# A two-block kernel on one core: ten of the twelve weight turns of the second attention taken from TensorE to VectorE and a pass through DRAM, and the level sums of the linear attention done earlier

## The chip, the cores and the metric

The kernel runs on one core of a Trainium2 chip. The metric is the time of one execution on the device, in microseconds; a lower time is better. All arithmetic is fp32; the large products are split into a high and a low part, so that each is three matmuls.

## What is computed

Two transformer blocks follow one another on 256 rows of 1024 columns. The first has a feed-forward part, a windowed attention with sinks beside a convolution, a second feed-forward part and a gated embedding. The second, cut to what matters here:

```python
h = rmsnorm(x) * (1 + sc2) + sh2
q_a, k_a, v_a, a_low, r_a, q_b, k_b, v_b, f_b, gate_a, gate_b = split(h @ w_in)
o_a = gla_chunked(q_a, k_a, v_a, log_a)          # linear attention, 4 heads of 128 x 256
o_b = fox_attention(q_b, k_b, v_b, logf)         # 16 heads of 64, causal:
#   s = q.k / 8 + F_t - F_s ; p = softmax(s) ; o = p @ v
merged = sigmoid(gate_a) * (o_a @ w_pa) + sigmoid(gate_b) * (o_b @ w_pb)
y = merged @ w_out
```

## The kernel before

**Stream of weight units.** All large products read weights as units of 128x1024 floats from DRAM. SyncE's queue loads them into a ring of eight buffers. ScalarE writes the high part `w_hi` (L676), VectorE the low part `w_lo` (L1194), TensorE multiplies (a unit of 512 columns is `col_unit`, L2029 to L2031, twelve matmuls) and frees the buffer. Each engine has one instruction list, written by hand, and steps through the units in the same order; `w.to(n)` in the lists of ScalarE and VectorE makes the parts of the units up to n + 1. Everything else is put between units.

**Second attention.** It runs in the sixteen steps of the last projection of the second mixer (the gate columns, a block of four units for each 512 columns; `for step in range(16)` at L1149, L1967, L2631). There are twelve groups of work, each with 128x512 scores in PSUM bank 4: groups 0 to 3 are four heads of the first 128 queries, groups 4 to 11 two heads of the second 128 queries with 256 keys. Group a has its scores at step a + 3:

- TensorE: `score_heads2` (L2285) adds q.k to the mask that ScalarE has copied into bank 4.
- VectorE: `heaviest2` takes the row maxima (L1533).
- ScalarE: `weigh2` takes the exponentials into `pr2` (L859) with their sums, then copies the next group's mask into bank 4 (L863).
- One step later TensorE turns the four 128x128 tiles of `pr2` into bank 5 (`turn_weights2`, L2295), ScalarE copies them to `pt2` (`take_turned2`, L870), and halfway through that step's unit TensorE multiplies them with the values, again into bank 5 (`weighted_values2`, L2306), as the stationary operand. VectorE scales and evicts the result (`take_values2`, L1545).

At steps 4 and 5 TensorE also turns the output of the linear attention.

**Linear attention.** Its scores are built up in nine steps, `gla_scores(i)` on TensorE and `masked(i)` on VectorE, one at the end and start of each block from 4 to 12 of the same projection. Steps 1 to 7 are levels of halving distance that are summed into `AT[:, 2]`; step 8 is the product between the two halves of the rows. When block 12 is over, TensorE turns the level sum (`turn_levels`, L2560) and issues step 8 (L2553). VectorE adds the sum to one diagonal tile, and the turned sum to the other (`add_levels`, two operations each, L1865 and L1866), and copies step 8 (L1846). `gla_values` (L2624), halfway through step 0 of the gate columns, needs all of that. Step 0 itself waits until ScalarE has evicted block 12 (L1127).

**GpSimd's queue** issues small loads, those of the modulation weights `ada` (L589), and in the second mixer the two rows of `Frow` (L665, L666). After these it has nothing until the last feed-forward part. The row-block layout that VectorE's transpose makes (32x32 blocks) is already used for the hidden units of the feed-forward parts (L1462), with DMAs on SyncE's queue that bring the blocks to their places.

## Time and profile before

| what | us |
|---|---|
| three runs | 1329.16, 1329.49, 1333.8 |
| median | 1329.49 |
| the profiled execution: its own time | 1329.29 |
| its span, from the first to the last instruction | 1327.5 |
| TensorE busy (share of the span) | 1311.3 (99%) |
| VectorE busy | 948.3 (71%) |
| ScalarE busy | 747.1 (56%) |
| GpSimd busy | 67.4 (5%) |

TensorE's clock was granted at 0.999 of full speed (2.4 GHz) over the span. The own time holds 1.8 us more than the span, which lies before the first and after the last instruction. In the rows, PE is TensorE's matmuls, PEld its weight loads (they overlap the matmuls), DVE is VectorE, ACT ScalarE, POOL GpSimd, SPq SyncE's queue of DMA issues; ps is PSUM. A matmul's duration in the rows includes its way through the pipeline, so that the spacing of the starts, not the duration, tells what it costs. The trace calls pr2, pt2 and gates2 by the names pr, pt and gates.

### The profile page before, as it was taken

What the parts mean: (1) busy time and instruction counts of PE and PEld (TensorE: products, weight loads), DVE (VectorE), ACT (ScalarE), POOL (GpSimd) and SP (SyncE); (2) the same over time, 40 slices, a digit from 0 to 9 for tenths busy, and PEclk for the clock granted to TensorE, in tenths of its full rate; (3) what the DMA queues carried; (4) which work ended last, traced back from release to release, by engine and by line L of the source; (5) the groups of instructions that cost most, each with busy time, mean ns of one, the idle gap of its engine ahead of it and who ended that gap; (6) DMA issues with size and microseconds to landing.
All of it is one profiled execution on the core that took longest, in us unless ns stands there. A gap on an engine that the chain in (4) does not pass through costs nothing.

```text
span 1327.5 us, 17135 instructions
## 1 busy us (share of the span) xinstructions
PE 1311.3 (99%) x6371; PEld 1094.0 (82%) x6371; DVE 948.3 (71%) x1352; ACT 747.1 (56%) x1149; POOL 67.4 (5%) x132
## 2 busy tenths in 40 slices
PE   9999999999999999999999999999999999999998
PEld 6888888888888888888788888889978888788886
DVE  6788877856656878887777888677866455766554
ACT  6454457567774544546744536766457663745452
POOL 3100100000000000110000010100000000000000
PEclk9999999999999999999999999999999999999999
DMA  9999966533375699895589996655644355567763
GB/s 288 317 297 310 319 215 191 174 114 109 96 254 184 212 277 311 306 338 160 173 252 298 294 309 183 204 175 173 172 133 119 104 175 173 159 207 217 219 197 105
DMA packets 185491, 282.45 MB, mean 213 GB/s; under 512 B 20386, under 2 KB 133258, under 8 KB 185408
## 3 DMA queue, kind: packets, MB, share of 16 engines
q1 hardware_dynamic: 172672, 238.22, 58.0%
q0 software_dynamic: 12576, 43.06, 9.8%
q8 instruction: 51, 0.84, 0.3%
q14 instruction: 32, 0.26, 0.1%
q10 hardware_dynamic: 160, 0.07, 0.1%
HBM read 268.66 MB, written 1.05 MB: 203 GB/s over the span
## 4 chain that ended last, share of the span: by engine, by line
PE 93%; DVE 3%; ACT 2%; DMA 1%; issue 0%; SPq 0%; DVEq 0%; POOL 0%; ACTq 0%
PE ps L2064 25%; PE ps L2029 16%; PE ps L2031 16%; PE ps L2030 16%; PE ps L2247 2%; PE ps L2043 1%; PE ps L2044 1%; PE ps L2045 1%; PE ps L2147 1%; PE ps L2149 1%; PE ps L2148 1%; PE ps L2079 1%; PE ps L2168 1%; PE ps L2322 1%; PE ps L2306 1%; PE ps L2285 1%
## 5 line engine op out<-in xcount | busy, mean ns | idle before, releaser
L1194 DVE TENSOR_TENSOR w_lo<-raw,w_hi 128x1024 fp32r<-128x1024 f32 (+2 forms) x431 | 514.2, 1213 | 218.1 <-ACT w_hi L676 216.8
L676 ACT ACTIVATE w_hi<-raw 128x1024 fp32r<-128x1024 f32 (+2 forms) x431 | 448.7, 1055 | 370.0 <-DMA raw<-in_w_gu_dram 100.0
L2029 PE MATMUL ps<-w_hi,a_hi 128*128 128x512 f32 (+1 forms) x976 | 386.4, 396 | 0.9 <-DVE w_lo L1194 0.9
L2031 PE MATMUL ps<-w_hi,a_lo 128*128 128x512 f32 (+1 forms) x976 | 378.7, 388 | 0.0
L2030 PE MATMUL ps<-w_lo,a_hi 128*128 128x512 f32 (+1 forms) x976 | 378.2, 387 | 0.0
L2031 PEld LDWEIGHTS ps<-w_hi,a_lo 128*128 128x128 f32 x976 | 183.3, 188 | 38.2
L2029 PEld LDWEIGHTS ps<-w_hi,a_hi 128*128 128x128 f32 x976 | 183.5, 188 | 36.8 <-DVE w_lo L1194 1.4
L2030 PEld LDWEIGHTS ps<-w_lo,a_hi 128*128 128x128 f32 x976 | 183.6, 188 | 35.7
L2064 PE MATMUL ps<-w_hi,hid_hi 128*128 128x512 f32 x300 | 93.1, 392 | 0.0
L2064 PE MATMUL ps<-w_hi,hid_lo 128*128 128x512 f32 x300 | 92.5, 389 | 0.0
L2064 PE MATMUL ps<-w_lo,hid_hi 128*128 128x512 f32 x300 | 92.4, 389 | 0.0
L1485 DVE SCALAR_TENSOR_TENSOR acc_m<-ada,csil,acc_m 128x1024 f32<-128x1024 f32 x63 | 80.7, 1281 | 4.7 <-DMA ada<-in_w_ada_dram 1.4
L2064 PEld LDWEIGHTS ps<-w_hi,hid_lo 128*128 128x128 f32 x300 | 56.3, 188 | 11.8
L2064 PEld LDWEIGHTS ps<-w_lo,hid_hi 128*128 128x128 f32 x300 | 56.3, 188 | 11.7
L2064 PEld LDWEIGHTS ps<-w_hi,hid_hi 128*128 128x128 f32 x300 | 55.7, 188 | 11.1
L589 POOL DMA_DIRECT2D ada<-in_w_ada_dram x72 | 38.3, 532 | 432.8 <-DVE acc_m L1485 269.3
L2064 PE MATMUL ps<-w_hi,a_hi 128*128 128x512 f32 x144 | 45.4, 396 | 0.6 <-DVE a_lo L1398 0.5
L2043 PE MATMUL ps<-a_hi,w_hi 128*128 128x256 f32 x160 | 45.9, 287 | 0.0
L2045 PE MATMUL ps<-a_lo,w_hi 128*128 128x256 f32 x160 | 45.3, 283 | 0.0
L2044 PE MATMUL ps<-a_hi,w_lo 128*128 128x256 f32 x160 | 45.3, 283 | 0.0
L2064 PE MATMUL ps<-w_lo,a_hi 128*128 128x512 f32 x144 | 44.4, 390 | 0.0
L2064 PE MATMUL ps<-w_hi,a_lo 128*128 128x512 f32 x144 | 44.4, 389 | 0.0
(438 smaller groups left out, 1597.0 us busy)
## 6 DMA issues: line engine op xcount, KB each, us to landing
raw<-in_ffn_wgu_dram SPq DMA_DIRECT2D x176, 256.0 KB, 4.7
raw<-in_w_in_dram SPq DMA_DIRECT2D x88, 512.0 KB, 3.7
raw<-in_w_gu_dram SPq DMA_DIRECT2D x176, 256.0 KB, 3.8
ada<-in_w_ada_dram POOLq DMA_DIRECT2D x72, 512.0 KB, 6.2
raw<-in_ffn_wdown_dram SPq DMA_DIRECT2D x44, 512.0 KB, 6.3
raw<-in_w_dn_dram SPq DMA_DIRECT2D x44, 512.0 KB, 4.6
raw<-in_w_in_dram SPq DMA_DIRECT2D x36, 256.0 KB, 3.1
raw<-in_w_out_dram SPq DMA_DIRECT2D x16, 512.0 KB, 3.7
```

What stands on the lines that cost most here:

```text
L589: pool.dma_start(ada[:, i % 3, :], w_ada[k, :, m * D:(m + 1) * D]).then_inc(sem(f"ada_landed{i % 3}"), 16)
L676: act.activation(w_hi[:, u % RING, 0:nk * n], raw[:, u % RING, 0:nk * n], ACT.Copy).then_inc(hi_ready, 1)
L1194: dve.tensor_tensor(w_lo[:, u % RING, 0:nk * n], raw[:, u % RING, 0:nk * n], w_hi[:, u % RING, 0:nk * n].bitcast(F32), ALU.subtract).then_ ...
L1485: ins = dve.scalar_tensor_tensor(acc_m[:, m % 2, :], ada[:, i % 3, :], csil[:, k:k + 1], acc_m[:, m % 2, :], ALU.mult, ALU.add)
L2029: pe.matmul(dst(t)[:, 0:n], a[0], slot(u, w_hi, kk, n), start=kc == 0, stop=False)
L2030: pe.matmul(dst(t)[:, 0:n], a[0], slot(u, w_lo, kk, n), start=False, stop=False)
L2031: i = pe.matmul(dst(t)[:, 0:n], a[1], slot(u, w_hi, kk, n), start=False, stop=kc == KC - 1)
L2043: pe.matmul(dst, hi, a_hi[:, kc, :], start=kc == 0 and q % 2 == 0, stop=False, skip_group_check=True)
L2044: pe.matmul(dst, lo, a_hi[:, kc, :], start=False, stop=False, skip_group_check=True)
L2045: i = pe.matmul(dst, hi, a_lo[:, kc, :], start=False, stop=kc == KC - 1, skip_group_check=True)
L2064: i = pe.matmul(ps[:, bank + 2 * t + n, :], a[x_], slot(u, w_, 0, D, 512 * n, 512 * (n + 1)), start=kc == 0 and x_ == 0 and w_ is w_hi, st ...
L2247: i = pe.matmul(ps[:, 2 * t + n, :], a[x_], slot(u + k, w_, 0, D, 512 * n, 512 * (n + 1)), start=k == 0 and x_ == 0 and w_ is w_hi, stop=F ...
```

## The change

Groups 0 to 9 of the second attention (`MOVED = 10`) are no longer turned on TensorE. In the step of their scores VectorE transposes `pr2` by 32x32 blocks into `blocks2`, written so that the four 128-column tiles lie interleaved. GpSimd's queue stores the 128x512 result in rows of the output tensor (which the kernel overwrites at its end), waits until the store has landed, and loads it back with four DMAs, one for each 32 partitions of `rows2`, where the blocks then stand as full transposes. TensorE reads them as the stationary operand, every fourth element, two steps after the scores and no longer one. Groups 10 and 11 keep the old way, with banks 6 and 7 for the turned tiles. ScalarE's evictions of turned tiles remain for those two. In the linear attention both `add_levels` move into block 12 on VectorE, and `turn_levels` between the second and the third unit of block 12 on TensorE. Semaphores of the two attentions are merged; this changes no order.

```diff
+        blocks2, _, _ = place("blocks2", [P, 2, 4, 32, 4], F32, KD0)
+        rows2, _, e = place("rows2", [P, 3, P, 4], F32, e)
+        def passed2(i):
+            return out[0, i % 2 * P:(i % 2 + 1) * P, 0:512]
+        MOVED = 10
...
+            for i in range(MOVED):
+                pool.wait_ge(sem("a2_blocks"), i + 1)
+                pool.dma_start(passed2(i), blocks2[:, i % 2].rearrange("p q v b -> p (q v b)")).then_inc(sem("a2_passed"), 16)
+                pool.wait_ge(sem("a2_passed"), 16 * (i + 1))
+                if i >= 1:
+                    pool.wait_ge(sem("a2_moved"), 64 * i)
+                if i >= 3:
+                    pool.wait_ge(sem("a2_values"), i - 2)
+                for q in range(4):
+                    dst = rows2[32 * q:32 * q + 32, i % 3].rearrange("p (i v) b -> p i (v b)", i=4)
+                    src = passed2(i).rearrange("(i u) (q n) -> q u i n", i=4, q=4)[q]
+                    pool.dma_start(dst, src).then_inc(sem("a2_moved"), 16)
...
-                if i >= 2:
-                    act.wait_ge(sem("a2_turned"), i - 1)
+                if 2 <= i < MOVED + 2:
+                    act.wait_ge(sem("a2_blocks"), i - 1)
...
-                if 1 <= a <= NG:
+                if MOVED < a <= NG:
                     take_turned2(a - 1)
...
+            def turn_blocks2(i):
+                dve.wait_ge(sem("a2_exp"), exps(i))
+                if i >= 2:
+                    dve.wait_ge(sem("a2_passed"), 16 * (i - 1))
+                dve.transpose(blocks2[:, i % 2].rearrange("p q v b -> p b q v"), pr2[:, i % 2, :].rearrange("p (b q u) -> p b q u", b=4, u=32))\
+                   .then_inc(sem("a2_blocks"), 1)
...
+                if b == 12:
+                    add_levels(0, AT[:, 2, :, :])
                 w.to(u1 + 2)
...
+                if b == 12:
+                    dve.wait_ge(sem("levels_turned"), 1)
+                    add_levels(1, by_head(ps[:, 5, :]))
                 w.to(u1 + 4)
...
                 w.to(G + step + 4)
-                if 1 <= a <= NG:
+                if 0 <= a < MOVED:
+                    turn_blocks2(a)
+                if 2 <= a < MOVED + 2:
+                    take_values2(a - 2)
+                if MOVED < a <= NG:
                     take_values2(a - 1)
...
             def weighted_values2(i):
                 n, h0, nh, nk = GROUPS[i]
+                if i < MOVED:
+                    pe.wait_ge(sem("a2_moved"), 64 * (i + 1))
+                    rows = [rows2[:, i % 3, :, c] for c in range(4)]
+                else:
+                    pe.wait_ge(sem("weights_taken"), NG + i - MOVED + 1)
+                    rows = [pt2[:, i % 2, c * P:(c + 1) * P] for c in range(4)]
                 if i >= 1:
                     pe.wait_ge(sem("a2_evict"), i)
...
+                    if b == 12 and i == 1:
+                        pe.wait_ge(sem("gla_masked"), NSTEP - 1)
+                        turn_levels()
...
-                if 1 <= a <= NG:
+                if MOVED < a <= NG:
                     turn_weights2(a - 1)
...
-                    if 1 <= a <= NG:
+                    if 2 <= a < MOVED + 2:
+                        weighted_values2(a - 2)
+                    if MOVED < a <= NG:
                         weighted_values2(a - 1)
```

## Rows read from the trace of the kernel before

**Rows 1.** The page: busy time of each engine and its share of the span.

```profile
PE 1311.3 (99%) x6371; PEld 1094.0 (82%) x6371; DVE 948.3 (71%) x1352; ACT 747.1 (56%) x1149; POOL 67.4 (5%) x132
```

**Rows 2.** Busy by stretch: us, engines, PEclk, DMA share, GB/s.

```profile
1000.00:1065.00 65.00, 64.69 (x383) 56.18 (x383) 35.91 (x74) 44.19 (x113) 0.00 (x0) 1.00 0.37 108
```

**Rows 3.** Groups by line: count | busy us, mean ns | idle before.

```profile
L2306 PEld LDWEIGHTS ps<-vb,pt 128*128 128x128 f32 x96 | 12.6, 191 | 1.0
...
L2295 PE MATMUL ps<-const,pr 128*128 128x128 f32 x48 | 7.3, 274 | 0.3 <-ACT pr L859 0.3
```

**Rows 4.** TensorE in time, steps 13, 14: start us, us, engine, line.

```profile
1051.41 1.03 PE L2285 MATMUL ps<-kb,qb 66*128 66x256 f32 x4
1052.09 0.58 PE L2029 MATMUL ps<-w_hi,a_hi 128*128 128x512 f32 x1
...
1053.65 1.00 PE L2306 MATMUL ps<-vb,pt 128*128 128x64 f32 x8
1054.45 0.48 PE L2029 MATMUL ps<-w_hi,a_hi 128*128 128x512 f32 x1
...
1055.92 0.60 PE L2295 MATMUL ps<-const,pr 128*128 128x128 f32 x4
...
1060.87 0.60 PE L2295 MATMUL ps<-const,pr 128*128 128x128 f32 x4
```

**Rows 5.** VectorE and ScalarE in order of time, steps 13 and 14.

```profile
1054.75 0.29 DVE L1545 TENSOR_TENSOR oat<-ps,st 128x128 f32<-128x128 f32 x1 [0.18 <-PE ps L2306]
1057.43 0.69 DVE L1533 TENSOR_REDUCE st<-ps 128x2 f32<-128x512 f32 x1 [2.38 <-PE ps L2285]
...
1058.82 0.47 ACT L859 ACTIVATE pr<-ps,st 128x256 f32<-128x256 f32 x1
```

**Rows 6.** Steps 3 and 4 in order of time, three engines.

```profile
1003.77 1.22 DVE L1194 TENSOR_TENSOR w_lo<-raw,w_hi 128x1024 fp32r<-128x1024 f32 x1
...
1004.24 0.60 ACT L863 ACTIVATE ps<-const 128x512 f32<-128x512 f32 x1
...
1004.89 1.16 PE L2285 MATMUL ps<-kb,qb 66*128 66x128 f32 x8
```

**Rows 7.** End of linear attention, in time; brackets: idle, its releaser.

```profile
983.25 0.60 PE L2560 MATMUL ps<-const,AT 128*128 128x128 f32 x4
983.45 1.09 ACT L1127 ACTIVATE vb<-ps 128x512 f32<-128x512 f32 x2 [0.47 <-PE ps L2031]
...
983.69 1.06 PE L2553 MATMUL ps<-qk 128*128 128x128 f32 x8
...
984.59 0.50 PE L2029 MATMUL ps<-w_hi,a_hi 128*128 128x512 f32 x1
...
987.05 0.69 DVE L1846 COPY AT<-ps 128x512 f32<-128x512 f32 x1
...
987.80 1.99 PE L2624 MATMUL ps<-va,AT 128*128 128x256 f32 x8 [1.56 <-DVE AT L1846]
```

**Rows 8.** VectorE's block transposes, one of two tiles: ns min/median/max.

```profile
L1462 DVE STREAM_TRANSPOSE turned_even<-hid x24: 711/712/715, 29.8 to 1252.9; 128x512 f32<-128x512 f32 x24
```

**Rows 9.** VectorE and GpSimd in order of time, from 869 us.

```profile
869.18 0.74 DVE L1923 TENSOR_SCALAR Frow<-ps 16x256 f32<-16x256 f32 x2
...
870.22 0.50 POOL L665 DMA_DIRECT2D qb<-Frow  x1 [32.95 <-DVE Frow L1923]
```

**Rows 10.** GpSimd's DMA issues, one line: ns min/median/max.

```profile
L589 POOL DMA_DIRECT2D ada<-in_w_ada_dram x72: 530/530/554, 33.1 to 793.1; - x72
```

**Rows 11.** DMA issues: count, KB each, median us issue to landing.

```profile
out_dram<-x SPq DMA_DIRECT2D x4, 256.0 KB, 2.0
...
glam<-shape_constants_dram POOLq DMA_DIRECT2D x1, 512.0 KB, 3.9
...
pin<-in_p_dram POOLq DMA_DIRECT2D x1, 256.0 KB, 4.6
...
qb<-Frow POOLq DMA_DIRECT2D x1, 16.0 KB, 2.1
```

More of the change, by code:

```diff
@@ L865, in take_turned2 @@
             def take_turned2(i):
-                act.wait_ge(sem("a2_turned"), i + 1)
-                if i >= 2:
-                    act.wait_ge(sem("a2_values"), i - 1)
-                act.activation(pt2[:, i % 2, :], ps[:, 5, :], ACT.Copy).then_inc(sem("a2_pt"), 1)
+                act.wait_ge(sem("weights_turned"), NG + i - MOVED + 1)
+                act.activation(pt2[:, i % 2, :], ps[:, 6 + i % 2, :], ACT.Copy).then_inc(sem("weights_taken"), 1)
             def split_hi(k):
@@ L930, in weigh @@
                     act.wait_ge(sem("qs_ready"), 2)
-                act.wait_ge(sem("a1_bias"), i + 1)
+                act.wait_ge(sem("bias_ready"), i + 1)
                 if i >= 2:
-                    act.wait_ge(sem("a1_turned"), i - 1)
+                    act.wait_ge(sem("weights_turned"), i - 1)
                 if i >= 4:
@@ L1553, in heaviest @@
                     dve.wait_ge(sem("qs_ready"), 2)
-                dve.wait_ge(sem("a1_scores"), i + 1)
+                dve.wait_ge(sem("scores_ready"), i + 1)
                 src = ps[:, 4, 0:nh * L].rearrange("p (h k) -> p h k", k=L)
@@ L2286, in score_heads2, with weighted_values2 @@
                                    skip_group_check=True)
-                i_.then_inc(sem("a2_scores"), 1)
+                i_.then_inc(sem("scores_ready"), 1)
             def turn_weights2(i):
                 pe.wait_ge(sem("a2_exp"), exps(i))
+                pe.wait_ge(sem("act_lo"), 8 * TURN["oa"] + 8)
+                for q in range(4):
+                    i_ = pe.transpose(ps[:, 6 + i % 2, q * P:(q + 1) * P], pr2[:, i % 2, q * P:(q + 1) * P], ident)
+                i_.then_inc(sem("weights_turned"), 1)
+            def weighted_values2(i):
+                n, h0, nh, nk = GROUPS[i]
+                if i < MOVED:
[4 more added lines that the diff above has]
+                    rows = [pt2[:, i % 2, c * P:(c + 1) * P] for c in range(4)]
                 if i >= 1:
                     pe.wait_ge(sem("a2_evict"), i)
-                for q in range(4):
-                    i_ = pe.transpose(ps[:, 5, q * P:(q + 1) * P], pr2[:, i % 2, q * P:(q + 1) * P], ident)
-                i_.then_inc(sem("a2_turned"), 1)
-            def weighted_values2(i):
-                n, h0, nh, nk = GROUPS[i]
-                pe.wait_ge(sem("a2_pt"), i + 1)
                 for q in range(nh):
@@ L2304, in weighted_values2 @@
                     for k in range(nk):
-                        c = (q * nk + k) * P
-                        i_ = pe.matmul(ps[:, 5, q * HD:(q + 1) * HD], pt2[:, i % 2, c:c + P], vb[:, k, hh * HD:(hh + 1) * HD],
+                        i_ = pe.matmul(ps[:, 5, q * HD:(q + 1) * HD], rows[q * nk + k], vb[:, k, hh * HD:(hh + 1) * HD],
                                        start=k == 0, stop=k == nk - 1)
@@ L2323, in score_heads @@
                                    start=False, stop=True, skip_group_check=True)
-                i_.then_inc(sem("a1_scores"), 1)
+                i_.then_inc(sem("scores_ready"), 1)
             def turn_weights(i):
@@ L2332, in turn_weights @@
                     i_ = pe.transpose(ps[:, 5, q * P:(q + 1) * P], pr[:, i % 2, q * P:(q + 1) * P], ident)
-                i_.then_inc(sem("a1_turned"), 1)
+                i_.then_inc(sem("weights_turned"), 1)
             def weighted_values(i):
                 n, h0, nh, nk = GROUPS[i]
-                pe.wait_ge(sem("a1_pt"), i + 1)
+                pe.wait_ge(sem("weights_taken"), i + 1)
                 for q in range(nh):
```

19 lines of the change are left out of this document (7 added, 12 removed).

## The prediction

> **What bounds the kernel.** I began with the page: TensorE is busy 99% of the span [rows 1]. A change can then win only by giving TensorE less to do or by closing one of its few gaps, and it loses wherever TensorE has to wait for something new. Next I took the busy times by stretch for the sixteen steps of the second block's gate columns, where the second attention runs: TensorE 64.69 of 65 us, VectorE 35.91, ScalarE 44.19, GpSimd nothing, DMA engines 0.37 [rows 2]. TensorE is the bound, and GpSimd and the DMA engines look free. The groups by line give the price of what is removed [rows 3], the order in time gives one steady step [rows 4] with the other engines beside it [rows 5], the first step [rows 6] and the end of the linear attention [rows 7]. For the new path there is nothing in this stretch, so I read, from the whole run, VectorE's block transposes, GpSimd's DMA issues and the list of landings [rows 8 to 11].
>
> One steady step [rows 4]: scores from 1051.41 to 1052.09 (0.68 us), half a weight unit to 1053.65 (1.56), weighted values to 1054.45 (0.81), the other half to 1055.92 (1.46), transposes to the next scores. The step before ends where the next begins, 1055.92 to 1060.87: 4.95 us.
>
> **Removed from TensorE.** Four transposes for each of ten groups. In the steady step they fill 1055.92 to 1056.36, as the rest of the step adds up to 4.51 of 4.95: 0.44 us a group (the group's 274 ns a transpose is pipelined duration, not spacing [rows 3]). Ten would be 4.4. The first gives nothing: at 1004.89 the scores of group 1 start right after ScalarE's mask copy ends (1004.24 + 0.60 = 1004.84) [rows 6], so without the transposes TensorE waits for that copy instead. Nine groups give 9 x 0.44 = 3.9 us. ScalarE's ten evictions go too, but ScalarE is not the bound: nothing.
>
> **Moved on TensorE.** The weighted values of groups 0 to 9 come one step later. The same matmuls, so no cost, but step 14 now holds those of group 9 and of group 10, and both write bank 5: the second waits until VectorE has evicted the first. In step 13 VectorE's eviction ends at 1054.75 + 0.29 = 1055.04, 0.6 after the values end at 1054.45 [rows 4, 5]; behind a whole weight subtraction (1.22 us [rows 6]) it would be about 1.2. I take **0.9 us lost**, between the two.
>
> **Added to VectorE.** Ten 128x512 block transposes. The nearest row is 712 ns for the same shape [rows 8]; this one writes each element 16 bytes from the last, which no row shows, so 0.71 to 1.42 (double). It waits for the group's last exponential, and behind it stand the eviction and the next group's maximum. Scores at 1056.36 give the maximum at 1057.43 (+1.07) and the last exponential until 1059.29 (+2.93) [rows 5]; transposed by +3.75, evicted by +4.4. The next maximum starts at 4.51 + 1.07 = +5.58, so 1.1 us is spare and the transposes are hidden; at 1.42 still just.
>
> **Added on GpSimd: the part that decides.** A group is one 256 KB store to DRAM, a wait until it has landed, and four 64 KB loads, all issued by one queue in order. The loads of a group also wait for those of the group before (landed by then, while a load takes under 3 us) and for a buffer. So GpSimd cannot take groups faster than
>
> period P = store landing (Lw) + wake (0.30) + 4 issues.
>
> Wake: VectorE finished Frow at 869.92 and GpSimd issued at 870.22 [rows 9]. An issue: 0.53 us, 72 of them between 530 and 554 ns [rows 10]. Lw is not shown. From below, 2.0 us: the 256 KB output stores on SyncE's queue when nothing else moves. On GpSimd's queue 16 KB landed in 2.1 us and 512 KB in 3.9; a straight line gives 3.0 at 256 KB. From above, 4.6 us: the 256 KB load of pin on that queue beside other traffic [rows 11]. Here the DMA engines are about a third busy [rows 2], so I take **2.7**, nearer the quiet rows. P = 2.7 + 0.3 + 2.12 = 5.12 us. TensorE's step without the transposes is 4.51. GpSimd is slower and sets the pace, and the pace is even slower than the 4.95 of before.
>
> The end of that chain: group 0's exponentials are done while VectorE is in the subtraction that ends at 1003.77 + 1.22 = 1004.99 [rows 6]; transposed 1005.7; first store issued 1006.0. Ten periods later the queue is at 1057.2, the last load was issued 0.53 before that and lands Lr later. Lr for 64 KB: the same line gives 2.3, from 2.1 (16 KB) to 3.9; I take 2.4 since four overlap. Landed 1059.07, TensorE starts group 9's values at 1059.2, then 0.81 + 0.9 + 0.81 + 1.46 brings step 14 to its end at 1063.2. Before it ended at 1060.87 [rows 4]. **Attention: +2.3 us.** While GpSimd paces, 0.1 us on Lw is worth 1.0 us on the end.
>
> The loads of weights share the DMA engines with this. Each is asked for several steps ahead and the engines are far from full, so nothing; uncovered, a late unit would stop TensorE directly. The DMAs pass nothing: GpSimd's next work lies after the attention, and the output rows used as scratch are written by SyncE at the very end.
>
> **Linear attention.** Before: the four level transposes at 983.25, scores of the last level to 984.59, step 0 begins, then gla_values waits 1.56 us until VectorE has done four level operations and the copy of 987.05 to 987.74 [rows 7]. After: the transposes sit inside block 12 (0.44 moved, not saved), the four operations of 0.69 run under its matmuls, where VectorE has pauses, and only the copy follows. It takes 0.69 and is done before the first half of step 0 is. So the 1.56 goes, but something else is late: step 0 also needs ScalarE's evictions of block 12, which start when its matmuls end, 983.45 to 984.54. Now they end 0.44 later, at 985.0, against 984.59 where step 0 began. 1.56 - 0.4 = **1.2 us gained**. Bounds: 0 (VectorE late with its subtractions) and 1.6.
>
> **Sum.** +2.3 - 1.2 = +1.1 on the profiled execution's own 1329.29 us (span 1327.5): 1330.4. The median of the runs is 0.2 above it, so **1330.6 us**. By 0.5% (6.65 us, about what a measurement of this kernel tells from no change) that is no change.
>
> **Rivals.**
>
> *The round trip keeps up.* With Lw at or under 2.3, as the output stores suggest, TensorE waits only for group 0 (0.2 us at Lw 2.1): -3.9 + 0.9 + 0.2 - 1.2 = -4.0, 1325.5 us. For it: stores may be quicker than loads. Against it: both GpSimd rows beyond 16 KB.
>
> *The store lands late: slower.* The same chain, but Lw 3.5 with the weight loads' bursts in the way, as pin's 4.6 hints [rows 11]: +1.1 + 8 = +9.1, 1338.6 us. It decides from Lw = 3.25 on (1.1 + 5.5 = 6.6). Against it: pin met other traffic that is mostly absent here.
>
> *The stationary operand is slow to load.* Group rows now lie interleaved, so each stationary column is 16 bytes after the last. In this stretch the value matmuls are spaced 0.1 us apart and their weight loads take about 0.19 each [rows 3, 4], so little hides a longer load. If the load takes twice as long, values cost 1.62 a group, a step 5.32: above GpSimd's 5.12, so the two do not add, TensorE is simply the slower one. 8.1 more on the -4.0 of the keeping-up case, with part of group 0's wait on top: about +5, 1334.6. At three times, +13. No row here has such a stride. The Trainium skill ("SBUF — State Buffer", Specifications) says SBUF has 16-byte lines and wants at least two hits on a line for full bandwidth; by it this stride of one hit a line is the bad case, on the stationary operand and on VectorE's write both. No trace here shows it.
>
> *GpSimd is held up while it issues.* If two of a group's five issues each waited 0.6 us for a VectorE operation, +12 on the chain, 1342.6. Against it: 72 issues at 530 to 554 ns beside a busy VectorE [rows 10]. The Trainium skill ("SBUF — State Buffer", SBUF: two separate sides) describes VectorE's two-port modes locking GpSimd out of writing descriptors; by that rule it is possible, and the trace shows no sign of it.
>
> **Chances.** The forecast (GpSimd paces, Lw 2.4 to 3.2, own range 1327.6 to 1335.6) 0.42; keeps up 0.20; late store 0.16; slow stationary load 0.17, a third of it at the triple price; held up 0.05. Faster by over 0.5% would need 6.65 us, and all gains together (4.4 + 1.6) do not reach it: 0.03 for what I overlook. Slower by over 0.5%: 0.16 + 0.06 + 0.05 and the edge of the forecast, 0.30. Same: 0.67. The range for 8 in 10 goes from 1325.0, just under the keeping-up case, to 1341.0, which takes in Lw up to 3.7 and leaves out the triple load and most of the held-up case.
>
> **What would show it.** On GpSimd, 50 issues, the stores 5.1 us apart with no pause but the wait for landing; store landing 2.7, load landing 2.4. On TensorE, no idle before the scores, a wait of about 1.5 before group 0's values and about 0.6 before each later group's, by DMA; in step 14 a wait by VectorE near 0.9; gla_values without its 1.56, and about 0.4 before step 0. Values at 0.1 us apart and weight loads at 0.19 refute the slow load. VectorE's block transpose at 0.71 or above tells the stride's price there. I am wrong if Lw is off by more than a few tenths, which weighs ten times over, or if the interleaved rows cost TensorE time of their own.

## The result and the profile after

The changed kernel takes 1348.01 us (median of 6 runs, 1346.66 to 1354.3) against 1329.59 for the kernel before on the same chip: ratio 1.014, 95% interval [1.0124, 1.0155], 18.4 us slower. The forecast was 1330.6 with a range of 1325.0 to 1341.0. It was wrong: the time lies 7 us above the range. The profiled execution took 1351.19 us (span 1349.4). Line numbers below are those of each kernel's own program, so the values of a group are L2306 before and L2341 after, the scores L2285 and L2315, a weight unit's matmuls L2029 to L2031 and L2059 to L2061.

As before, the busy times by stretch come first; the stretch of the sixteen gate steps now ends near 1087. The columns are us, busy time of PE, PEld, DVE, ACT, POOL, granted clock as a share of 2.4 GHz, share of the DMA engines and GB/s.

```profile
1010.00:1020.00 10.00, 7.93 (x37) 6.66 (x35) 4.57 (x10) 3.99 (x15) 4.97 (x10) 0.83 0.54 162
...
1030.00:1040.00 10.00, 6.84 (x25) 5.61 (x24) 3.53 (x6) 4.51 (x9) 5.46 (x10) 0.79 0.51 150
...
1070.00:1080.00 10.00, 6.39 (x25) 5.49 (x24) 2.62 (x7) 1.60 (x5) 0.61 (x2) 0.67 0.24 70
1080.00:1090.00 10.00, 9.70 (x45) 7.89 (x45) 3.01 (x7) 3.73 (x8) 0.00 (x0) 0.82 0.37 107
```

Before, TensorE was busy 64.69 of 65 us at full clock here [rows 2]. Now these three windows from 1010 to 1080 have 2 to 3.6 us without TensorE, and in the same windows the clock is down to 0.67 to 0.83: for a part of them TensorE ran at the lower of its two levels, 1.2 GHz. Next, who waited for whom on TensorE, 984 to 1090 us: us in total, times, longest.

```profile
PE ps L2341 <- DMA rows<-out_dram: 8.3, 3, 3.2
PE ps L2315 <- ACT ps L881: 1.0, 1, 1.0
PE ps L2341 <- DVE oat L1569: 0.5, 1, 0.5
```

The groups of the new path in 984 to 1088 us (count | busy, mean ns of one | idle before):

```profile
L684 POOL DMA_DIRECT2D rows<-out_dram x40 | 21.8, 551 | 30.4 <-DMA out_dram<-blocks 29.7 <-issue 0.6
L2341 PEld LDWEIGHTS ps<-vb,rows 128*128 128x128 f32 x80 | 19.4, 325 | 10.1 <-DMA rows<-out_dram 9.8
L1557 DVE STREAM_TRANSPOSE blocks<-pr 128x512 f32<-128x512 f32 x10 | 11.1, 1115 | 1.3 <-ACT pr L877 1.3
```

A stationary load of landed rows takes 325 ns where it took 191 [rows 3]; a block transpose that writes every 16 bytes takes 1115 ns where 712 is the kernel's other price [rows 8]. GpSimd's issue is 0.55 us as expected [rows 10]. And TensorE in order of time, around the first long wait:

```profile
1010.82 0.40 PE L2061 MATMUL ps<-w_hi,a_lo 128*128 128x512 f32 x1
1013.29 2.08 PE L2341 MATMUL ps<-vb,rows 128*128 128x64 f32 x8 [2.07 <-DMA rows<-out_dram]
1015.18 0.60 PE L2059 MATMUL ps<-w_hi,a_hi 128*128 128x512 f32 x1
1015.58 0.63 PE L2060 MATMUL ps<-w_lo,a_hi 128*128 128x512 f32 x1
1016.00 0.63 PE L2061 MATMUL ps<-w_hi,a_lo 128*128 128x512 f32 x1
...
1019.93 0.48 PE L2059 MATMUL ps<-w_hi,a_hi 128*128 128x512 f32 x1
1020.25 0.40 PE L2060 MATMUL ps<-w_lo,a_hi 128*128 128x512 f32 x1
1020.48 0.39 PE L2061 MATMUL ps<-w_hi,a_lo 128*128 128x512 f32 x1
```

Behind a wait of 2.07 us the matmuls start 0.42 us apart (1015.58 to 1016.00) instead of 0.23 (1020.25 to 1020.48), until 1019. The other two waits, 3.16 and 3.06 us, are followed by the same picture; the lower clock is granted for 3.4, 6.8 and 10.2 us. Last, GpSimd in order of time, and one weight load of SyncE:

```profile
1016.13 0.56 POOL L675 DMA_DIRECT2D out_dram<-blocks  x1
1018.75 2.17 POOL L684 DMA_DIRECT2D rows<-out_dram  x4 [2.06 <-DMA out_dram<-blocks]
1025.02 0.58 POOL L675 DMA_DIRECT2D out_dram<-blocks  x1 [4.10 <-DVE blocks L1557]
1031.31 2.31 POOL L684 DMA_DIRECT2D rows<-out_dram  x4 [5.71 <-DMA out_dram<-blocks]
```

```profile
1024.71 0.37 SPq L541 DMA_DIRECT2D raw<-in_w_in_dram  x1
```

The store of 1016.13 lets GpSimd go on 2.6 us later, that of 1025.02 6.3 us later. The second one was issued 0.31 us behind a 512 KB weight load. That store is what TensorE's 3.16 us at 1035.46 come from. Over the ten stores the landing has this spread:

```profile
DMA to landing us min/median/max: 2.3/2.4/6.0
```

The three waits do not have one origin. Group 0's store (1005.62) landed in the quick 2.34 us. Its last row load was issued at 1009.9, so even a landing of 2.3 us would have come 1 us after TensorE was ready at 1011.2; it took 3.4 us, which makes the 2.07. The wait before group 9's values closes a chain of two late stores and a late row load, here in the order of the chain that ends there (start, us):

```profile
1056.53 4.15 DMA out_dram<-blocks
...
1063.13 5.03 DMA out_dram<-blocks
...
1070.06 4.20 DMA rows<-out_dram
...
1074.31 1.90 PE ps L2341 x7
```

The linear attention did what the prediction said:

```profile
984.34 1.05 PE L2588 MATMUL ps<-qk 128*128 128x128 f32 x8
985.67 0.50 PE L2059 MATMUL ps<-w_hi,a_hi 128*128 128x512 f32 x1 [0.28 <-ACT vb L1143]
...
987.17 1.02 PE L2660 MATMUL ps<-va,AT 128*128 128x256 f32 x4
```

The 1.56 us ahead of the values [rows 7] are gone and 0.28 stand before step 0.

### The profile page after: what moved, and what is told of

It is laid out like the page before. It is cut to its first block, busy times and chain, and to the rows that moved or that the text cites. A ratio compares the mean times of both kernels' runs of the same rounds, so it can differ in the third digit from the quotient of the medians.

```text
span 1349.4 us, 17117 instructions
## 1 busy us (share of the span) xinstructions
PE 1324.3 (98%) x6331; PEld 1104.8 (82%) x6331; DVE 957.5 (71%) x1362; ACT 741.1 (55%) x1139; POOL 94.5 (7%) x182
## 4 chain that ended last, share of the span: by engine, by line
PE 89%; DMA 4%; DVE 3%; POOL 1%; ACT 1%; issue 1%; SPq 0%; DVEq 0%; ACTq 0%; POOLq 0%
PE ps L2094 25%; PE ps L2059 15%; PE ps L2061 15%; PE ps L2060 15%; DMA out_dram<-blocks 2%; PE ps L2277 2%; PE ps L2073 1%; PE ps L2074 1%; PE ps L2075 1%; POOL rows L684 1%; PE ps L2177 1%; PE ps L2179 1%; PE ps L2178 1%; PE ps L2109 1%; PE ps L2198 1%
## 5 line engine op out<-in xcount | busy, mean ns | idle before, releaser
L2059 PE MATMUL ps<-w_hi,a_hi 128*128 128x512 f32 (+1 forms) x976 | 388.5, 398 | 1.3 <-DVE w_lo L1210 1.0
L2061 PE MATMUL ps<-w_hi,a_lo 128*128 128x512 f32 (+1 forms) x976 | 380.4, 390 | 0.0
L2059 PEld LDWEIGHTS ps<-w_hi,a_hi 128*128 128x128 f32 x976 | 184.8, 189 | 38.1 <-DVE w_lo L1210 1.5
L2061 PEld LDWEIGHTS ps<-w_hi,a_lo 128*128 128x128 f32 x976 | 184.4, 189 | 38.4
```

The source lines that it names most:

```text
L2059: pe.matmul(dst(t)[:, 0:n], a[0], slot(u, w_hi, kk, n), start=kc == 0, stop=False)
L2061: i = pe.matmul(dst(t)[:, 0:n], a[1], slot(u, w_hi, kk, n), start=False, stop=kc == KC - 1)
```

## The experiments

For every kernel I read the same distance in TensorE's order of time, from the scores of group 0 to the transposes of the second attention's output ("attention" in the table): 64.8 us before, 87.2 after. The profiled executions differ by 21.9 us (the changed kernel's is 3 us above its median), so all of the loss lies there. "Waits" are TensorE's for landed rows (us, times), "low" is the time at the lower clock inside the stretch, "store" the landing of the ten stores (min/median/max).

| kernel | median us | ratio [95%] | attention | waits | low | store |
|---|---|---|---|---|---|---|
| before | 1329.6 | | 64.8 | | 0 | |
| after | 1348.0 | 1.0140 [1.0124, 1.0155] | 87.2 | 8.3, 3 | 20.5 | 2.3/2.4/6.0 |
| levels | 1328.95 | 0.9993 [0.9984, 1.0002] | 64.8 | | 0 | |
| attn | 1349.5 | 1.0149 [1.0131, 1.0167] | 82.7 | 7.5, 3 | 10.2 | 2.3/3.0/4.7 |
| strided | 1340.0 | 1.0075 [1.0059, 1.0090] | 75.3 | | 0 | |
| contig | 1350.0 | 1.0142 [1.0123, 1.0160] | 86.4 | 12.5, 4 | 27.3 | 2.3/3.5/4.7 |
| fill | 1343.8 | 1.0110 [1.0082, 1.0138] | 82.5 | 5.7, 3 | 10.2 | 2.3/2.9/4.5 |
| traffic | 1328.6 | 0.9993 [0.9984, 1.0003] | 64.9 | | 0 | 2.3/2.9/4.8 |
| gated | 1342.3 | 1.0097 [1.0082, 1.0112] | 78.7 | 3.6, 3 | 6.8 | 2.3/3.1/4.1 |
| gated_contig | 1340.7 | 1.0085 [1.0069, 1.0102] | 76.0 | 10.1, 9 | 3.4 | 2.3/3.1/4.2 |
| sp_loads | 1341.8 | 1.0089 [1.0074, 1.0104] | 78.1 | 3.6, 3 | 6.8 | 2.3/2.8/5.9 |
| late | 1335.3 | 1.0046 [1.0032, 1.0061] | 70.0 | 0 | 0 | 2.3/2.9/4.5 |
| late_contig | 1331.9 | 1.0011 [1.0000, 1.0022] | 65.1 | 2.2, 3 | 0 | 2.3/2.9/4.6 |
| late_scalar | 1339.7 | 1.0079 [1.0062, 1.0096] | 76.7 | 9.8, 9 | 6.8 | 2.3/2.9/5.1 |
| lead3 | 1336.6 | 1.0050 [1.0034, 1.0065] | 72.3 | 0 | 3.4 | 2.3/2.5/4.6 |
| lead3_scalar | 1335.6 | 1.0044 [1.0032, 1.0057] | 70.5 | 0 | 6.8 | 2.3/2.8/4.6 |

Each ratio is against runs of the kernel before on the same chip (medians 1329.35 to 1329.75 us). The attention, waits, low and store columns are of one profiled execution each, the median of 4 to 11 runs, and the two can differ by some us (attn: profiled 1347.66, median 1349.5), so a single trace places the loss only to about that. In late_scalar the waits are those for ScalarE's copy of the rows.

**The two halves of the change (levels, attn).** levels is the kernel before with only this:

```diff
+                if b == 12:
+                    add_levels(0, AT[:, 2, :, :])
...
+                    if b == 12 and i == 1:
+                        pe.wait_ge(sem("gla_masked"), NSTEP - 1)
+                        turn_levels()
...
-                    if b - 4 == NSTEP - 1:
-                        turn_levels()
```

> The kernel before with the level sums of the linear attention inside the last block and nothing else changed. Theory: the level sums are worth what the trace after shows, gla_values 1.3 us earlier after the last unit of block 12, at the price of nothing: about 1328.4 us, 0.999 of before. TensorE idle before gla_values gone, about 0.3 us before step 0. Rival: the gain is given back later (the first scores wait for the same chain on VectorE), 1329.6 us.

1328.95, and 1328.89 with 0.9991 [0.9982, 1.0000] in a second trial (levels2, below): 0.8 us under the kernel before on the same chip both times, while both intervals reach up to no change. A small gain is likely and not shown. attn is the changed kernel with the level sums put back after block 12 (the same lines the other way round).

> The changed kernel with the level sums put back behind the last block, so the attention part alone. Theory: this part carries the whole loss, about 1.3 us above the changed kernel: 1349 us (+19.7). Rival: part of the loss comes from the level sums, which delay VectorE: then this is at or under 1347 us.

1349.5: the whole loss is the attention's, whatever the linear attention does.

**The stride alone (strided).** The kernel before, but ScalarE writes its copy of the turned weights interleaved and TensorE reads them with 16 bytes from column to column. No store, no load, no wait.

```diff
-                act.activation(pt2[:, i % 2, :], ps[:, 5, :], ACT.Copy)
+                act.activation(pt2[:, i % 2, :].rearrange("p (v b) -> p b v", b=4), ps[:, 5, :].rearrange("p (b v) -> p b v", b=4), ACT.Copy)
...
-                        c = (q * nk + k) * P
+                        c = q * nk + k
```

> The kernel before with one edit: ScalarE writes the turned tiles into pt2 interleaved by four, and TensorE reads them as stationary operand with that stride of 16 bytes; no DMA, no block transposes. Theory: the stride alone costs 0.85 us for each of twelve groups, 10.2 us: 1339.8 us, weight loads at about 325 ns, clock as before. Rival: the slow weight loads of the changed kernel come from rows that a DMA has written or from traffic at the same time: then 1330 us and loads at 191 ns. ScalarE's strided write may be slower than 0.60 us, which is off TensorE's path.

```profile
L2306 PEld LDWEIGHTS ps<-vb,pt 128*128 128x128 f32 x96 | 23.3, 324 | 0.6 <-ACT pt L870 0.2
```

324 ns, and 10.3 us more for twelve groups, 0.86 a group, at full clock. The prediction's price for a slow stationary load (0.81 more a group) was nearly right. ScalarE's interleaved copy itself took 1097 ns where the contiguous one took 604.

**The stride taken out of the changed kernel (contig).** Here TensorE reads contiguous columns of the landed rows; the values are then computed with weights in another order, so that part of the computation is changed.

```diff
-                    rows = [rows2[:, i % 3, :, c] for c in range(4)]
+                    rows = [rows2[:, i % 3].rearrange("p a b -> p (a b)")[:, c * P:(c + 1) * P] for c in range(4)]
```

> The changed kernel, but TensorE reads the landed rows as four contiguous runs of 128 columns and not every fourth element. The weights it multiplies are then in the wrong order, so the attention's values are wrong; instructions, waits and DMAs are the same. Theory: the stride of 16 bytes makes a stationary load take 325 ns and not 191, which is 0.85 us for a group and 8.5 us in ten. Weight loads back at about 190 ns, values of a group in 0.81 us. GpSimd's queue then sets the pace (store 2.4, wake 0.3, four issues 2.2: 4.9 us a group against 4.51 on TensorE), so not all of the 8.5 us comes back; with some late stores and low clock left, 1337 us (1333 to 1341). Rival: waits for landings and the low clock after them carry the loss and the stride only fills time in which TensorE would have waited: over 1344 us.

My theory fell and the rival won: 1350.0 instead of 1337.

```profile
PE ps L2341 <- DMA rows<-out_dram: 12.5, 4, 4.0
```

Without the stride TensorE waits 12.5 us instead of 8.3 and the clock is low for 27.3 us instead of 20.5. The stride's 8.7 us were only filling time in which TensorE would have waited. What ruled was the wait for the landed rows and the clock after it. From here on the question was why the rows come late and what a wait costs.

**Is the clock a consequence of the wait? (fill)** Eight matmuls that nothing uses stand ahead of the first group's values, where TensorE waited 2.07 us.

```diff
+                if i == 0:
+                    busy(8, 5)
                 if i < MOVED:
                     pe.wait_ge(sem("a2_moved"), 64 * (i + 1))
```

> The changed kernel with eight dummy matmuls of 512 columns (about 1.8 us at full clock) on TensorE ahead of the first group's values, where it waits 2.07 us for the landed rows: the wait is filled with work that nothing uses. The theory of the clock: the low stretch at 1010 us and the matmuls at half speed behind it are gone, some 1.7 to 2 us, while the fill costs at most 0.3; what comes later (late stores at their own moments) may fall differently by some microseconds, so the total is 1345 to 1349 and the verdict rests on the window 1010 to 1020. Rival, the low clock has nothing to do with the wait ahead of it: the low stretch at 1010 stays and the time is 1348 to 1350.

```profile
1010.45 1.90 PE L2204 MATMUL ps<-maskD,identb 128*128 128x512 bf16 x8
1012.71 2.08 PE L2343 MATMUL ps<-vb,rows 128*128 128x64 f32 x8 [0.36 <-DMA rows<-out_dram]
1014.59 0.48 PE L2059 MATMUL ps<-w_hi,a_hi 128*128 128x512 f32 x1
...
1016.93 1.06 PE L2315 MATMUL ps<-kb,qb 66*128 66x128 f32 x8
```

1343.8, under the 1345 to 1349 expected; that later stores fell differently is my guess, and the four runs lie between 1341.0 and 1349.3. The values still start when the rows land, but the low stretch is gone: from the values to the next scores it is 4.22 us (1012.71 to 1016.93), in the changed kernel 5.83 (1013.29 to 1019.12). Dummy work of 1.9 us thus gave 1.6 us back. Granted clock in the window 1010 to 1020:

```profile
1010.00:1020.00 10.00, 9.64 (x52) 7.67 (x50) 6.03 (x14) 4.71 (x18) 4.74 (x10) 1.00 0.58 182
```

It was 0.83 in the changed kernel. Where the other waits were left as they are, the clock fell again (window 1030 to 1040: 0.66). The Trainium skill (TensorE: Matmul & The Clock Gate, Part 1) says that the gate follows how busy TensorE has just been; by that rule, the trace agrees.

**Does the round trip itself cost, and why are stores late? (traffic)** The kernel before with levels, and on top the block transposes, stores and loads of ten groups, for whose rows nobody waits: TensorE turns its weights as before.

```diff
+                if 0 <= a < MOVED:
+                    turn_blocks2(a)
...
+            for i in range(MOVED):
+                pool.wait_ge(sem("a2_blocks"), i + 1)
+                pool.dma_start(passed2(i), blocks2[:, i % 2].rearrange("p q v b -> p (q v b)")).then_inc(sem("a2_passed"), 16)
```

> The kernel before with level sums inside the last block, and on top the block transposes on VectorE and GpSimd's stores and loads of ten groups, for whose landed rows nobody waits: TensorE turns the weights as before and stays in its own pace. The store landings can then be read without TensorE's waits moving the weight loads. The theory: a store is late only where a weight load was issued within about 1 us of it; TensorE keeps full clock, and the time is that of the kernel before plus 0 to 3 us (VectorE's 1.1 us a step beside its splits): 1329 to 1333. Rival, the traffic itself costs (weight loads late, splits late, evictions held by block transposes): over 1337 us with TensorE waiting for VectorE or for landed weights.

1328.6: VectorE's, GpSimd's and the DMA engines' extra work is free. And the stores are late here too, with TensorE in its own even pace:

```profile
1046.42 0.56 POOL L675 DMA_DIRECT2D out_dram<-blocks  x1
1051.54 2.17 POOL L684 DMA_DIRECT2D rows<-out_dram  x4 [4.56 <-DMA out_dram<-blocks]
1053.70 0.56 POOL L675 DMA_DIRECT2D out_dram<-blocks  x1
```

SyncE had issued a weight load at 1045.77, 0.65 us ahead. I took all 80 stores of eight kernels (after, attn, contig, fill, traffic, lead3, gated, gated_contig) and read the time since SyncE's last recorded weight load, and from the store's issue until GpSimd issues again, which is the landing and some 0.3 us:

| last weight load | stores | until the next issue, median | over 3.2 us |
|---|---|---|---|
| up to 1.8 us before | 11 | 4.9 | 11 |
| 1.8 to 2.6 us | 27 | 3.5 | 21 |
| 2.6 to 3.0 us | 7 | 3.0 | 3 |
| over 3.0 us | 35 | 2.7 | 9 |

A few loads are missing from the records, which blurs the last row. Each of the 11 stores of the first row landed 0.5 to 1.2 us after the weight load that was issued ahead of it. Two of the nine late ones of the last row (contig, 3.6 and 4.7 us) have a weight load issued 0.2 to 0.3 us behind them.

Of the others, one in the changed kernel was issued at 1056.53 and took 4.15 us. While it was under way the DMA engines also moved one packet of 16 KB on the queue that the profile calls "instruction" (transfers from 1056.5 to 1060.7):

```profile
q8 instruction: 1, 0.02, 2.2%
```

Such packets come every 20 to 34 us in this stretch and take 0.9 to 1.7 us. In 10 of the 80 stores one began within 2.3 us of the store's issue, and all 10 landed late, in 3.45 to 4.6 us: six of the nine in the last row, and also the longest one of gated. So there is a second cause beside the weight loads as far as the traces tell; no run varies it, and the table is a count over traces, not an experiment.

**Keeping the weight loads out of the stores' way (gated, gated_contig).** SyncE holds a weight load until the group's store has landed.

```diff
+                if 0 < u - u_mix2[13] - 10 <= MOVED:
+                    sp.wait_ge(sem("a2_passed"), 16 * (u - u_mix2[13] - 10))
```

> SyncE issues the weight load that follows a step of this stretch only when the store of that step's group has landed (ten loads, each held by some 2.4 us; they are needed seven steps later). The theory: the store's landing, 2.3 us by itself, is late (3.3 to 6.0) where a 512 KB weight load was issued just ahead of it or beside it; each late store opens a wait of TensorE and each wait is followed by a stretch at half the clock. Then all ten stores land in 2.2 to 2.8 us, TensorE waits for landed rows at most 2 to 3 us in all, at the first groups, one low stretch of 3.4 us is left at most, and the time is that of the kernel before plus the stride (8.5 us) less the transposes (4.4) and the level sums' part (0.8), plus wait and clock (3 to 5): 1336 to 1341 us. Rival one, landings scatter by themselves or by the row loads: landings up to 4 or 6 us again, 7 to 10 us of waits, 1346 to 1350 us. Rival two, the held weight loads come late themselves: TensorE waits for split weights, over 1345 us.

1342.3, 5.7 us less than the changed kernel, a little above the theory's range. The longest landing fell to 4.1 (the one with the instruction packet), the longest wait to 1.9, the low time from 20.5 to 6.8 us. But the median landing rose to 3.1 and that of the row loads from 2.5 to 3.5: now the held weight loads meet the row loads and the next store. The collision was moved more than removed.

> The held weight loads and TensorE reading contiguous columns of the landed rows (the values are then those of other weights: this part of the computation is changed). With both suspected costs gone, what the prediction summed should be left: TensorE's step is 4.95 less 0.44 us, GpSimd's period 4.8 to 5.3 us paces, so waits of 0.3 to 0.8 us come in most steps, too short to lower the clock. The theory: 1328 to 1335 us, clock 1.00 in nearly every window. Rival (the waits and the clock don't hang on the late stores): waits of 2 to 4 us after landed rows as in the kernel with contiguous columns alone, clock under 0.9 in several windows, 1340 to 1350 us.

The time is the rival's, 1340.7, the picture neither's: the waits are many and short (9 with 10.1 us, longest 1.7) and the clock fell once. Without the stride TensorE's step is 4.5 us, and GpSimd's stores start 4.8 to 6.8 us apart, 5.5 at the median, so it paces.

**More time between a store and its use.** In sp_loads SyncE issues the row loads. It waits for the group's store before it does, and its weight load stands behind them, so sp_loads holds the weight load as gated does; its partner for comparison is gated. late is sp_loads with one thing more: in late the values of a moved group also come at the end of the step instead of in its middle, 2.3 us later.

```diff
+                if 0 <= u - u_mix2[13] - 11 < MOVED:
+                    load_rows2(u - u_mix2[13] - 11)
```

```diff
-                    if 2 <= a < MOVED + 2:
-                        weighted_values2(a - 2)
...
                 col_unit(G + step, 2 * i, lambda t: acc(t, b % 2), midway=midway)
+                if 2 <= a < MOVED + 2:
+                    weighted_values2(a - 2)
```

> SyncE issues the four row loads of a group as soon as its store has landed, and then its weight load; GpSimd issues only the stores. An issue on SyncE took 0.34 to 0.37 us in the changed kernel, on GpSimd 0.55, so a group's rows are under way 0.8 us sooner and GpSimd's 2.2 us of issues no longer separate two stores. TensorE still reads the strided rows. The theory (the rest of the loss is the chain store, loads, values, in which TensorE's step is only just longer than GpSimd's period, plus the clock after the longest waits): waits for rows fall from the 3.6 us of the gated kernel to 1 to 3, one low stretch or none: 1335 to 1340 us. Rival, what counts is contention of the transfers and not who issues them: landings of 3 to 5 us for store and loads remain, waits of 3 to 6 us, 1340 to 1345.

> As the kernel in which SyncE issues the row loads, with the values of the moved groups at the end of the step instead of between its two half units, 2.3 us later. The theory: no wait of TensorE for landed rows over 1 us and full clock in all windows; what is left is the stride (10 groups by 0.85 = 8.5 us) less the transposes (4.4) and the level sums (0.8): 1330 plus 3.3, with two groups in one step at the end 0.5 more: 1332 to 1336 us. Rival: the time stays at 1338 to 1343 although the waits are gone; then something not in this sum costs.

sp_loads gives the rival's 1341.8: row loads landed in 2.0 us, but stores still took up to 5.9, and 3.6 us of waits stayed, as in gated: who issues the loads made 0.5 us. late is at 1335.3, 6.5 us under sp_loads, as the theory had it, with stores up to 4.5 us:

```profile
1028.82 1.85 PE L2348 MATMUL ps<-vb,rows 128*128 128x64 f32 x8
1030.51 1.08 PE L2322 MATMUL ps<-kb,qb 66*128 66x256 f32 x4
...
1034.18 1.85 PE L2348 MATMUL ps<-vb,rows 128*128 128x64 f32 x8
...
1039.54 1.75 PE L2348 MATMUL ps<-vb,rows 128*128 128x64 f32 x7
```

No wait for rows at all, steps of 5.36 us. That is the step before (4.95) less the transposes (0.46) and plus the stride (0.87), and ten such steps with the 0.7 us of the fourth step's longer wait for the mask and 0.55 for two groups in one bank make 64.8 - 4.6 + 8.7 + 1.25 = 70.2 us; read are 70.0. late_contig is late with the reading of contig (again weights in another order).

> As late, with TensorE reading contiguous columns of the landed rows (the values are then those of other weights: this part of the computation is changed). Only now, with waits and low clock gone, should the stride show in the time: 8.5 us less than late, so 1324 to 1328 us. Rival: contiguous reading gives nothing here either (GpSimd or the transfers pace TensorE at 5.4 us a group, as in the gated kernel with contiguous columns): waits for rows in most steps, 1331 to 1338.

1331.9, the lower edge of the rival's range. The waits, though, are in three steps and not in most. Steps without a wait are 4.49 us (1038.91, 1043.40 and 1047.89 for the values), but at that pace TensorE overtakes the rows again in three of them.

```profile
1023.83 1.10 PE L2348 MATMUL ps<-vb,rows 128*128 128x64 f32 x8 [0.68 <-DMA rows<-out_dram]
1029.43 1.10 PE L2348 MATMUL ps<-vb,rows 128*128 128x64 f32 x8 [0.84 <-DMA rows<-out_dram]
...
1038.91 1.00 PE L2348 MATMUL ps<-vb,rows 128*128 128x64 f32 x8
1043.40 1.00 PE L2348 MATMUL ps<-vb,rows 128*128 128x64 f32 x8
1047.89 1.00 PE L2348 MATMUL ps<-vb,rows 128*128 128x64 f32 x8
```

So the stride's 8.7 us cost 3.4 us of median here and nothing in the changed kernel. late_scalar has ScalarE copy the landed rows into contiguous weights:

```diff
+                act.wait_ge(sem("a2_moved"), 64 * (i + 1))
+                act.activation(flat2[:, i % 2], rows2[:, i % 3].rearrange("p a b -> p b a"), ACT.Copy).then_inc(sem("a2_flat"), 1)
```

> As late, but ScalarE copies each group's landed rows into contiguous weights (as before it copied the turned ones out of PSUM), and TensorE reads the copies. The rows' chain grows by this copy, 0.6 to 1.2 us. The theory: the 2.3 us gained by the later values cover it: loads of stationary operands back at 190 ns, 1325 to 1329 us, the fastest so far. Rival: the copy comes too late or holds ScalarE's splits and exponentials, TensorE waits for it 0.5 to 1 us in most steps: 1330 to 1338.

The rival, and worse: 1339.7, TensorE waits for the copy in nine steps, up to 2.1 us, and the clock falls twice. The copy reads with the stride and takes 1.11 us in a chain that had no room for it.

**A whole step more (lead3, lead3_scalar, levels2).** lead3 leaves all issuing on GpSimd as in the changed kernel and takes the values of a moved group three steps after its scores, not two; the last two groups are then done behind the tenth in the last step.

```diff
-                    if 2 <= a < MOVED + 2:
-                        weighted_values2(a - 2)
+                    if 3 <= a < MOVED + 3:
+                        weighted_values2(a - 3)
```

> The changed kernel, stores and loads issued by GpSimd as there, but the values of a moved group three steps after its scores instead of two (the last two groups, turned by TensorE, wait for the tenth and are done in the last step with it). The theory: the late stores stay (landings up to 4 to 6 us), but each has 5.4 us more before TensorE asks for the rows, so no wait for rows over 1 us and no low clock; what is left is stride less transposes, and 1 us for three groups through one bank in the last step: 1333.5 to 1337 us. Rival (GpSimd's chain is longer than TensorE's step of 5.36 us on average, so it falls behind and the waits come later in the stretch): 2 to 6 us of waits in the last groups, 1338 to 1344.

1336.6, the theory's number. GpSimd's order shows a store as late as any:

```profile
1021.23 0.58 POOL L675 DMA_DIRECT2D out_dram<-blocks  x1
1026.11 2.31 POOL L684 DMA_DIRECT2D rows<-out_dram  x4 [4.31 <-DMA out_dram<-blocks]
1028.41 0.56 POOL L675 DMA_DIRECT2D out_dram<-blocks  x1
```

and TensorE never waits for rows. This one edit takes 11.4 us of the loss away, with landings of up to 4.6 us left as they are: a late landing costs only where the time between store and use is too short for it. lead3_scalar adds SyncE's issuing and ScalarE's copy to it.

> The same lead, row loads issued by SyncE, and ScalarE's copy of the landed rows into contiguous weights before TensorE reads them. The theory: with 2.3 us more than in late_scalar, whose longest wait was 2.1, the waits end; transposes gone (10 by 0.46 us) and the level sums' 0.8 less, 1.1 us for the three groups in the last step and 0.6 for the longer wait for the mask in the fourth: 1325.5 to 1328.5 us, the fastest of all. Rival, ScalarE and the transfers pace TensorE at over 4.95 us a step: 1329 to 1334.

> The kernel before with the level sums inside the last block alone, beside lead3_scalar on one chip: 0.3 to 0.9 us under the kernel before.

The rival's range, just over it: 1335.6. The stride is gone and no wait for rows is left, but ScalarE now has the copy as well as its splits, exponentials and mask copies. TensorE waits for ScalarE's mask copy in five steps (3.4 us), and in the last step, with three groups in one bank, once 2.29 us for the eviction, after which the clock falls for 6.8 us:

```profile
PE ps L2333 <- ACT ps L889: 3.4, 5, 1.2
PE ps L2359 <- DVE oat L1586: 2.8, 2, 2.3
```

No version of the attention part beats the kernel before. The only kernels under it are levels and traffic, which contains levels, both by less than 0.1% and inside the interval.

## Why the prediction was wrong

The loss inside the attention, 87.2 - 64.8 = 22.4 us, falls into these terms, read from the runs and from differences between their traces. It is an account of where TensorE's time went, not of what each edit would give back: contig removes the stride and gains nothing. Transposes gone -4.6. Stride +8.7. Mask and two groups in one bank +1.25. That is late, 70.0 us. Waits for rows +8.3. Slow clock: 1.6 after the first wait (against fill), 8.13 - 5.36 = 2.8 after the second (values at 1035.46 to values at 1043.59, against late), 12.26 - 9.08 = 3.2 after the third (values at 1074.31 to the output's transposes at 1086.57, against gated, 1068.47 to 1077.55), together 7.6. The sum is 85.9 of 87.2. Of the missing 1.3 us some 0.2 stand behind the first wait: the values after it take 1.88 us at full clock too (fill, 1012.71 to 1014.59), and 1.66 without a wait. The rest I did not settle.

In the forecast's own terms its +2.3 for the attention were -3.9 for the transposes, +0.9 for the shared bank and 5.3 of waits for rows. Measured are -3.9 (4.6 less the 0.7 at the mask), +0.55 and 8.3. What the sum put at nothing is the larger part: 8.7 for the stride and 7.6 for the clock.

- **Removed from TensorE: right.** 0.44 us a group forecast, 0.46 read from the steps (4.95 to 4.49). That group 0 gives nothing because of the mask copy was right too: a wait of 0.97 instead of 0.31.
- **Moved: right in kind.** 0.9 forecast for two groups in one bank, 0.55 measured.
- **Added to VectorE: hidden, as said.** 1.1 us each, inside the range of 0.71 to 1.42 (traffic costs nothing).
- **"GpSimd is slower and sets the pace": the step that failed.** "P = Lw + wake + 4 issues" is a correct sum (undisturbed: 2.6 + 2.2 = 4.8 us), and "I take 2.7" lay above the median landing of 2.4. But it was compared with a TensorE step of 4.51 us; with the stride, which the sum had at nothing, the step is 5.37 us (values at 1048.96 and 1054.33). GpSimd was then the quicker one, and seven of the ten groups (1, 2 and 4 to 8) have no wait for rows at all, where the forecast had about 0.6 us in each. The second mistake was to use one value for the landing. Landings run from 2.3 to 6.0; the ten from a store's issue to GpSimd's next have a mean of 3.5 us in the changed kernel, and the formula's sum for it was 3.0. A mean doesn't tell the cost either. With the values due two steps after the scores, a late landing is not averaged away: it opens a wait of its own (3.16 us behind the store of 6.0, 3.06 behind two late stores and a late row load), and the quick stores beside it give nothing back. The 2.07 us before group 0 are another matter: its store was quick, about 1 us of it is the chain's own length, and a wait of about 1.5 had been forecast there. Given a step more, stores of up to 4.6 us cost no wait at all (lead3).
- **"The loads of weights share the DMA engines with this ... so nothing": wrong.** I looked only at whether a weight load would come late. It was the store that did, behind the packets of a weight load issued just ahead: all of the 11 stores within 1.8 us of one. The instruction packets, which the prediction does not mention, go with 10 late stores, one of them among those 11.
- **The missing term: the clock.** No line of the prediction gives a price to a wait beyond its own length. Three waits of 8.3 us cost some 7.6 us more through matmuls at the lower clock; only the first part of it (1.6) is shown by an experiment, the other two are differences between executions. The kernel before has one wait of 1.56 us, ahead of the linear attention's values, with the clock staying at 1.00, and only 0.31 in this stretch, and I didn't ask what happens to an engine that has been 99% busy when it is not.
- **The rivals.** *The store lands late* named the mechanism (chance 0.16), with 1338.6; it lacked the clock, and the stride beside it. *The stationary operand is slow to load* had the price right (1.66 a group measured, 1.62 said) and also the sentence "the two do not add": contig and the changed kernel take the same time. *Keeps up* held for those seven groups and not for the other three. *Held up while it issues* is not borne out: the row loads' issues took 548 to 566 ns, with one pause of 0.56 us among all 50 issues. The Trainium skill (SBUF — State Buffer, Specifications) was cited for 16-byte lines and one hit a line as the bad case; by that rule, the runs agree: 324 ns for 191 on the stationary operand, 1.11 us for 0.71 on VectorE's write.
- **Linear attention: right in size, hardly visible.** In the trace the gap of 1.56 became 0.28, a gain of 1.28 (1.2 forecast); in whole runs levels gives 0.8 us, inside the interval of no change.

## What to carry to other kernels

A round trip through DRAM that is short enough on the median can still set the pace: lay out its time of use for the latest landing seen beside the kernel's other traffic (here 6 us for 256 KB, behind a 512 KB load), not for the median, and add a step of lead before doing anything about who issues what. A wait of 2 us or more on a TensorE that was busy all the time cost nearly double here, since the matmuls behind it ran at the lower clock for some us. A cost measured alone (the stride, +10.3) tells nothing of its share in a kernel that waits anyway, so take waits out first and then price the rest.

## What the runs showed of the hardware

- A stationary operand with 16 bytes from column to column loads in 324 to 325 ns instead of 191; eight such loads and their 64-column matmuls take 1.66 to 1.69 us instead of 0.81 to 0.83. A 128x512 block transpose writing at that distance takes 1.11 us instead of 0.71, ScalarE's 128x512 copy 1.10 instead of 0.60.
- A 256 KB store on GpSimd's queue landed in 2.3 us at best and in 3.4 to 6.0 where a 512 KB weight load had been issued up to 1.8 us before (11 stores), and in 3.45 to 4.6 where a 16 KB packet of the instruction queue began within 2.3 us of its issue (10 stores). The 64 KB row loads landed in 2.0 to 2.2 us at the median when SyncE issued them, in 2.4 to 3.6 when GpSimd did; what else was under way differs between these kernels too.
- After the changed kernel's waits of 2.07 to 3.16 us TensorE's granted clock was at the lower level for 3.4 to 10.2 us. A wait of 1.14 us (gated) was followed by it too, waits of 1.6 to 1.7 us (gated_contig) once in four times and one of 1.58 us in late_scalar as well, single waits of up to 0.97 us never, but two of 0.54 us close together at the end of lead3 were. Filling a wait of 2.07 us with 1.9 us of dummy matmuls kept it up.
- Traffic of 5 MB more through VectorE, GpSimd and the DMA engines in 60 us cost a TensorE-bound kernel nothing as long as nothing waited for it (0.9993 [0.9984, 1.0003]).
